# Layer 0 of a diffusion trunk: its first eight projection units on the input before normalisation, and the square sums in the third block

## The chip, the cores and the metric

The kernel runs on one core of one Trainium2 chip. The time is the device time in microseconds (us) of one execution, as a median over several. Five engines work side by side and meet only at semaphores: TensorE (PE, with its weight load PEld), VectorE (DVE), ScalarE (ACT), GpSimd (POOL) and SyncE (SP), which here issues nearly all transfers (DMA).

## The reference, cut to what matters

Two layers run over 128 context tokens and 256 latent tokens, 384 columns in all. Each begins so:

```python
mod = silu(cond) @ w_ada + b_ada              # (2, 6144): one row for each kind of token
sh1, sc1, g1, sh2, sc2, g2 = split(mod, 6)
h = x * rsqrt(mean(x*x) + EPS) * g_norm1 * (1 + sc1) + sh1
u = h @ w_in                                  # columns feed four mixers and their gates
```

Write s for g_norm1 * (1 + sc1), which differs per channel, and r for the reciprocal root, which differs per token. Since r is one number per token, h @ W equals r * ((x*s) @ W) + sh1 @ W. The product can so be made before r is known, if sh1 @ W is computed beside it (two columns, one for each kind of token). All products keep 32-bit accuracy by splitting each operand into a high and a low part and adding three matmuls: high*high, low*high and high*low.

## The kernel before, in words

Channels lie on the 128 partitions, in 8 blocks k of 128; tokens are the 384 free columns. A projection unit is 128 output columns: 8 blocks times 3 matmuls of 384 columns. Layer 0 has 13 mixing units: xa0, xa1, q0, q1, xc0, xc1, k0, k1, then v0 and v1 (made together in `values`, with the token tiles as weights), cq, ckv, cqr. 32 gate units follow.

**The head of layer 0.** Its first 7 units (SKIP) are computed side by side in banks 0 to 6, block by block, as their inputs arrive. For each block j there are two transfers: `start_ada` j (1024 KB of modulation weights: shift and scale of channel block j; 6 buffers, so the seventh waits for a buffer) and `start_raw` j (448 KB, the weights of 7 units for that block). SP issues them alternately, behind the condition, the ones, the input x in two halves, and the small parameters.

PE runs `start_squares` (11 warm-up matmuls on the ones, then the square sums of x in two halves), `start_modulate(0)`, `start_modulate(1)`, then for each j `start_products(j)` (7 high*high, then 14 with a low part) and `start_modulate(j + 2)`. A modulation is 32 matmuls, each with a weight of 32 columns, into bank 7; the trace shows 64 records for it.

DVE squares half of x and adds the squares before it. In `start_norm(j)` it transposes the modulation out of bank 7, adds the bias (`mod`), makes s (`sc1`), multiplies x*s*r into `wide`, splits the weights (`start_low`), and makes the low part of h. ACT squares the other half, computes r from the square sums (`roots`: Ln, then Exp), makes the high part of the weights (`start_high`) and of h (`normed_high`). POOL has nothing to do in the head.

**After the head.** Unit 7 (k1) runs through the general path `dense` on the normalised high and low parts `ahi`, `alo`, and then `values(8)` runs three token tiles. ACT copies the units' sums out of their banks into `proj` and signals `mix_out`; the first tile asks only for one of them, the third for `mix_out` of 8 units in the changed and unchanged code alike. POOL's window sums start on units 0 and 1. The streamed weights pass through 4 buffers (`w_raw` to `w_hi` by ACT, to `w_lo` by DVE).

**Layer 1 already has the scheme of the change.** Its first 8 units run on the unnormalised x*s with two more columns for the shift; `rescale` on DVE multiplies each unit's sums with r and copies the two columns out, `add_shift` on ACT adds them, and POOL multiplies x*s by r for the units that come later (`normed`). Its rows in the trace show what these operations take.

## Time and profile before

| | us |
|---|---|
| median of 3 runs | 1218.28 (1217.79 to 1218.54) |
| the profiled execution's own time | 1218.61 |
| its span | 1216.7 |
| PE busy | 1200.5 (99% of the span) |
| DVE busy | 946.3 (78%) |
| ACT busy | 601.4 (49%) |
| POOL busy | 147.1 (12%) |

The span runs from the first to the last recorded instruction; the execution's own time is 1.9 us more. PE's busy share says only that it had an instruction under way: matmuls overlap, and the step from one start to the next says what one costs. What the order of the work is worth is read from the waits and from the start times.

### The profile page before, as it was taken

What the parts mean: (1) busy time and instruction counts of PE and PEld (TensorE: products, weight loads), DVE (VectorE), ACT (ScalarE), POOL (GpSimd) and SP (SyncE); (2) the same over time, 40 slices, a digit from 0 to 9 for tenths busy, and PEclk for the clock granted to TensorE, in tenths of its full rate; (3) what the DMA queues carried; (4) which work ended last, traced back from release to release, by engine and by line L of the source; (5) the groups of instructions that cost most, each with busy time, mean ns of one, the idle gap of its engine ahead of it and who ended that gap; (6) DMA issues with size and microseconds to landing.
All of it is one profiled execution on the core that took longest, in us unless ns stands there. A gap on an engine that the chain in (4) does not pass through costs nothing.

```text
span 1216.7 us, 19749 instructions
## 1 busy us (share of the span) xinstructions
PE 1200.5 (99%) x7688; PEld 1146.8 (94%) x7688; DVE 946.3 (78%) x1751; ACT 601.4 (49%) x1023; POOL 147.1 (12%) x125
## 2 busy tenths in 40 slices
PE   7999999999999999999999999999999999999998
PEld 6987999989989999999999889999999999999998
DVE  5588877848689999988867978787687899999532
ACT  3445564542365555543446545646437764454321
POOL 0222000008200000000132500000271200000000
PEclk9999999999999999999999999999999999999999
DMA  9763433544744455457673644343325444454443
GB/s 369 295 221 124 145 116 119 173 140 156 259 167 147 156 161 169 155 186 245 217 263 108 222 138 139 105 128 115 104 88 186 144 132 145 156 165 148 138 139 122
DMA packets 53821, 200.91 MB, mean 165 GB/s; under 512 B 6816, under 2 KB 7232, under 8 KB 51936
## 3 DMA queue, kind: packets, MB, share of 16 engines
q1 hardware_dynamic: 53408, 198.96, 48.2%
q8 instruction: 62, 1.02, 0.3%
q0 software_dynamic: 320, 0.69, 0.2%
q14 instruction: 31, 0.25, 0.1%
HBM read 197.35 MB, written 2.27 MB: 164 GB/s over the span
## 4 chain that ended last, share of the span: by engine, by line
PE 95%; DVE 2%; DMA 1%; issue 1%; ACT 0%; SPq 0%; DVEq 0%
PE bank L1602 27%; PE bank L1604 27%; PE bank L1603 27%; PE bank L1920 1%; PE bank L1900 1%; PE bank L1670 1%; DMA start_ada<-start_ada 1%; DVE w_lo L1077 1%; PE bank L1675 1%; PE bank L1674 1%; PE bank L1890 1%; PE bank L1659 1%; PE bank L1875 1%; DMA ada<-ada_w 1%; PE bank L1724 0%
## 5 line engine op out<-in xcount | busy, mean ns | idle before, releaser
L1602 PE MATMUL bank<-act_hi,w_hi 128*128 128x384 f32 x1240 | 421.9, 340 | 0.1
L1604 PE MATMUL bank<-act_hi,w_lo 128*128 128x384 f32 x1240 | 415.0, 335 | 0.0
L1603 PE MATMUL bank<-act_lo,w_hi 128*128 128x384 f32 x1208 | 403.9, 334 | 0.0
L1077 DVE TENSOR_TENSOR w_lo<-w_raw,w_hi 128x1024 fp32r<-128x1024 f32 x251 | 324.5, 1294 | 97.4 <-ACT w_hi L673 96.5
L673 ACT ACTIVATE w_hi<-w_raw 128x1024 fp32r<-128x1024 f32 x251 | 264.2, 1053 | 159.4 <-DMA w_raw<-stream 159.3
L1602 PEld LDWEIGHTS bank<-act_hi,w_hi 128*128 128x128 f32 x1240 | 233.1, 188 | 8.7 <-issue 5.3
L1604 PEld LDWEIGHTS bank<-act_hi,w_lo 128*128 128x128 f32 x1240 | 232.7, 188 | 0.0
L1603 PEld LDWEIGHTS bank<-act_lo,w_hi 128*128 128x128 f32 x1208 | 226.9, 188 | 0.6
L1602 PE MATMUL bank<-mlp_hi,w_hi 128*128 128x384 f32 x352 | 118.3, 336 | 0.0
L1604 PE MATMUL bank<-mlp_hi,w_lo 128*128 128x384 f32 x352 | 118.3, 336 | 0.0
L1603 PE MATMUL bank<-mlp_lo,w_hi 128*128 128x384 f32 x352 | 118.3, 336 | 0.0
L673 ACT ACTIVATE mlp_tmp<-bank,params 128x384 f32<-128x384 f32 x88 | 54.7, 667 | 73.4 <-PE bank L1604 73.1
L1492 DVE SCALAR_TENSOR_TENSOR mlp_tmp<-bank,params,mlp_tmp 128x127 f32<-128x127 f32 (+1 forms) x176 | 64.7, 409 | 16.0 <-ACT mlp_tmp L673 16.0
L1496 DVE SCALAR_TENSOR_TENSOR mlp_tmp<-bank,params,mlp_tmp 128x127 f32<-128x127 f32 (+1 forms) x176 | 65.2, 412 | 3.1
L1602 PEld LDWEIGHTS bank<-mlp_hi,w_hi 128*128 128x128 f32 x352 | 66.2, 188 | 0.1
L1603 PEld LDWEIGHTS bank<-mlp_lo,w_hi 128*128 128x128 f32 x352 | 66.2, 188 | 0.0
L1604 PEld LDWEIGHTS bank<-mlp_hi,w_lo 128*128 128x128 f32 x352 | 66.2, 188 | 0.0
L1108 DVE SCALAR_TENSOR_TENSOR row_products_mix<-ada,cond_spread_mix 128x1024 f32<-128x1024 f32 x44 | 56.4, 1282 | 5.0 <-DMA cond_spread_mix<-cond_rows 3.2
L673 ACT ACTIVATE gates_b<-bank 128x384 f32<-128x384 f32 x48 | 23.6, 492 | 64.0 <-PE bank L1604 63.7
L1363 DVE TENSOR_REDUCE small<-bank 128x1 f32<-128x384 f32 (+1 forms) x72 | 31.2, 462 | 28.3 <-PE bank L1878 11.1
L662 POOL TENSOR_TENSOR wide<-wide 128x768 f32<-128x768 f32 x8 | 18.6, 2330 | 273.7 <-DVE wide L1431 273.7
L1602 PE MATMUL bank<-merged_hi,w_hi 128*128 128x384 f32 x128 | 43.4, 339 | 4.0 <-DVE w_lo L1077 3.6
(261 smaller groups left out, 1866.0 us busy)
## 6 DMA issues: line engine op xcount, KB each, us to landing
w_raw<-stream SPq DMA_DIRECT2D x251, 512.0 KB, 3.7
ada<-ada_rows SPq DMA_DIRECT2D x64, 512.0 KB, 4.7
start_ada<-start_ada SPq DMA_DIRECT2D x8, 1024.0 KB, 17.9
ada<-ada_w SPq DMA_DIRECT2D x8, 512.0 KB, 5.5
ada_norm<-ada_w SPq DMA_DIRECT2D x8, 512.0 KB, 5.8
start_raw<-start_w SPq DMA_DIRECT2D x8, 448.0 KB, 18.5
cond_spread_mix<-cond_rows SPq DMA_DIRECT2D x2, 1024.0 KB, 8.6
cond_spread<-cond_rows SPq DMA_DIRECT2D x2, 1024.0 KB, 7.7
```

What stands on the lines that cost most here:

```text
L662: own(nc.gpsimd.tensor_tensor(g[:, 0:2, :], g[:, 0:2, :], g[:, 2:4, :], ALU.add))
L673: return nc.scalar.activation(out, in_, func, **kw)
L1077: V.tensor_tensor(wlo[s][:, :], raw[s][:, :], whi[s][:, :].bitcast(F32), ALU.subtract).then_inc(lo_ready, 1)
L1108: V.scalar_tensor_tensor(out[:, :], ada[b % 2][:, :], 1.0, tile[:, t, :], ALU.mult, ALU.mult, accum_out=mod[:, at, t:t + 1]).then_inc(rows ...
L1363: own(V.reduce_max(small[:, c + m:c + m + 1], bank[score_bank(i, m)][:, 0:n], AX))
L1492: own(V.scalar_tensor_tensor(f[:, m, a + 1:e], b[:, a:e - 1], before, f[:, m, a + 1:e], ALU.mult, ALU.add))
L1496: ins = V.scalar_tensor_tensor(f[:, m, a:e - 1], b[:, a + 1:e], behind, f[:, m, a:e - 1], ALU.mult, ALU.add)
L1602: T.matmul(out, wb[s][0][:, w, :], hi[k], start=first and k == 0, stop=False)
L1603: T.matmul(out, wb[s][0][:, w, :], lo[k], start=False, stop=False)
L1604: ins = T.matmul(out, wb[s][1][:, w, :], hi[k], start=False, stop=last and k == n - 1)
L1659: ins = T.matmul(bank[7][p0:p0 + STRIP, j * n:(j + 1) * n], conds[:, k, :], w[:, c:c + n], start=k == 0, stop=k == KD - 1)
L1670: T.matmul(outs[u], start_hi[j][:, cols[u]], HI[j], start=j == 0, stop=False)
```

## The change: what it does

- The 7 side-by-side units, and unit 7 behind them, use x*s without r (`suhi`, `sulo`, 386 columns: 384 and the two of the shift). `start_rescale` (DVE) and `start_add_shift` (ACT) finish all 8 units after the head.
- ACT makes x*s (`late`) and its high part, DVE its low part. POOL adds up the squares and then multiplies x*s by r for the later units; ACT and DVE make `ahi`, `alo` of these blocks from the fourth block on (START_NORMED).
- The square sums move on PE from ahead of the head to between the high and the low products of the third block, as one matmul into bank 7 (it was four into bank 4). All squares are ACT's.
- SP issues the parameters and `start_ada` 0 ahead of the input; the input goes in four quarters, with the blocks. `start_ada` has 3 buffers instead of 6.
- PE runs modulation 0, high products 0, modulation 1, low products 0, then modulation 2, high and low products 1, and so on. DVE makes the high weights of block 0, ACT the others. Modulation 4 waits for r, which ACT reads out of the same bank. 10 warm-up matmuls instead of 11.

```diff
-START_ADA = 6
-WARM = 11
+START_ADA = 3
+WARM = 10
+START_UNITS = SKIP + 1
+START_NORMED = {3: (0,), 4: (1, 2), 5: (3,), 6: (4, 5), 7: (6,)}
...
+            def load_input(h):
+
+                c0, c1 = 2 * h * TOK, (2 * h + 2) * TOK
+                sp.dma_start(x_t[:, c0:c1], x_in[:, c0:c1]).then_inc(x_loaded[h], 16)
...
-            for h in range(2):
-                c0, c1 = h * KD // 2 * TOK, (h + 1) * KD // 2 * TOK
-                sp.dma_start(x_t[:, c0:c1], x_in[:, c0:c1]).then_inc(x_loaded[h], 16)
             sp.dma_start(par[:, 0:HEAD_PARAMS], params[0:1, :, 0:HEAD_PARAMS].rearrange("a p n -> (a p) n")
                          ).then_inc(head_par_loaded, 16)
             for j in range(KD):
+                if 1 <= j < KD // 2:
+                    load_input(j)
                 if j >= START_ADA:
                     sp.wait_ge(ada_done, 2 * (j - START_ADA + 1))
                 sp.dma_start(start_ada_buf[j % START_ADA][:, :], start_ada[j:j + 1, :, :].rearrange("a p n -> (a p) n")
                              ).then_inc(start_ada_loaded[j % START_ADA], 16)
+                if j == 0:
+                    load_input(j)
                 sp.dma_start(start_raw[j][:, :], start_w[j:j + 1, :, :].rearrange("a p n -> (a p) n")
...
+                if l == 0:
+                    for h in range(KD // 2):
+                        pool.wait_ge(start_sq, h + 1)
+                        own(nc.gpsimd.tensor_tensor(wide[:, 2 * h, :], wide[:, 2 * h, :], wide[:, 2 * h + 1, :], ALU.add))
+                        own.wait()
+                        if h >= 1:
+                            own(nc.gpsimd.tensor_tensor(wide[:, 0, :], wide[:, 0, :], wide[:, 2 * h, :], ALU.add))
+                            own.wait()
+                    nc.gpsimd.sem_inc(start_sq_sum, 1)
+                    pool.wait_ge(rstd_ready, 1)
+                    for k in range(KD):
+                        pool.wait_ge(start_full, k + 1)
+                        nc.gpsimd.tensor_tensor(wide[:, k, :], late[:, k, :], rsn, ALU.mult).then_inc(norm_full, 1)
...
-            for h in range(2):
-                act.wait_ge(x_loaded[h], 16)
-                A(wide[:, 4 * h:4 * h + 2, :], x[:, 4 * h:4 * h + 2, :], ACT.Square).then_inc(start_sq_act, 1)
...
-                    own(A(rsn, bank[SUM_BANK[n + (l and n)]][:, 0:TOK], ACT.Ln, scale=1.0 / D, bias=EPSC))
+                    sums = bank[SUM_BANK[n + (l and n)]][:, 0:TOK] if l + n else bank[7][:, P:P + TOK]
+                    own(A(rsn, sums, ACT.Ln, scale=1.0 / D, bias=EPSC))
...
+                def start_square(h):
+
+                    act.wait_ge(x_loaded[h], 16)
+                    A(wide[:, 2 * h:2 * h + 2, :], x[:, 2 * h:2 * h + 2, :], ACT.Square).then_inc(start_sq, 1)
+
+                def start_unnormed_high(j):
+
+                    act.wait_ge(start_shift, j + 1)
+                    if j % 2 == 0 and j < 4:
+                        act.wait_ge(x_loaded[j // 2], 16)
+                    for a, e, c in RANGES:
+                        ins = A(late[:, j, a:e], x[:, j, a:e], ACT.Copy, scale=sc1[:, j, c:c + 1])
+                    ins.then_inc(start_full, 1)
+                    A(suhi[:, j, TOK:start_width], mod[:, j, :], ACT.Copy)
+                    act.wait_ge(start_full, j + 1)
+                    A(suhi[:, j, 0:TOK], late[:, j, :], ACT.Copy).then_inc(start_u_hi, 1)
+
+                def start_add_shift(q):
+
+                    out = pj[:, PJ[MIX[q]], :]
+                    act.wait_ge(start_rescaled, q + 1)
+                    for a, e, c in RANGES:
+                        ins = A(out[:, a:e], out[:, a:e], ACT.Identity, bias=start_sums[:, q, c:c + 1])
+                    ins.then_inc(mix_out, 1)
...
-                    norm(0)
-                    for u in range(SKIP, SKIP + 3):
-                        split(u)
+                    for j in range(KD):
+                        if j >= 1:
+                            start_high(j)
+                        if j == KD // 2 - 1:
+                            roots(0)
+                        start_unnormed_high(j)
+                        for h in ((0, 1), (2, 3))[j] if j < 2 else ():
+                            start_square(h)
+                        for k in START_NORMED.get(j, ()):
+                            normed_high(0, k)
+                    split(SKIP)
+                    normed_high(0, KD - 1)
+                    split(SKIP + 1)
+                    split(SKIP + 2)
+                    for q in range(START_UNITS):
+                        start_add_shift(q)
+                        if MIX[q] in SQUARED:
+                            mix_squares(q)
...
-            for h in range(2):
-                dve.wait_ge(x_loaded[h], 16)
-                xs = x[:, 4 * h + 2:4 * h + 4, :]
-                V.tensor_tensor(wide[:, 4 * h + 2:4 * h + 4, :], xs, xs, ALU.mult).then_inc(start_sq_dve, 1)
-                dve.wait_ge(start_sq_dve, h + 1)
-                dve.wait_ge(start_sq_act, h + 1)
-                V.tensor_tensor(wide[:, 4 * h:4 * h + 2, :], wide[:, 4 * h:4 * h + 2, :], wide[:, 4 * h + 2:4 * h + 4, :],
-                                ALU.add).then_inc(start_sq_sum, 1)
...
+                    if l + n == 0:
+                        dve.wait_ge(start_u_lo, k + 1)
...
-                    dve.wait_ge(start_w_hi, j + 1)
...
-                def start_norm(j):
+                def start_unnormed_low(j):
 
                     c0 = j * 2 * STRIP
-                    turned_block = rt_t[:, c0:c0 + 2 * STRIP].rearrange("p (b c) -> p b c", c=STRIP)
+                    turned_block = start_turned_t[:, c0:c0 + 2 * STRIP].rearrange("p (b c) -> p b c", c=STRIP)
                     dve.wait_ge(ada_done, 2 * (j + 1))
-                    turn = V.transpose(rt_t[:, c0:c0 + 2 * STRIP], bank[7][:, c0:c0 + 2 * STRIP])
+                    turn = V.transpose(start_turned_t[:, c0:c0 + 2 * STRIP], bank[7][:, j % 2 * 2 * STRIP:(j % 2 + 1) * 2 * STRIP])
                     if j < KD - 1:
                         turn.then_inc(start_read, 1)
                         dve.wait_ge(start_read, j + 1)
                     else:
                         turn.then_inc(mod_read, 2)
                         dve.wait_ge(mod_read, FROM + 2)
-                    V.tensor_tensor(mod[:, j:2 * KD:KD, :], turned_block[:, :, 0:2],
-                                    pc("b_ada", 0, 2 * KD)[:, j:2 * KD:KD].unsqueeze(2).to_broadcast([P, 2, 2]), ALU.add
-                                    ).then_inc(start_shift, 1)
-                    dve.wait_ge(start_shift, j + 1)
-                    own(V.scalar_tensor_tensor(sc1[:, j:j + 1, :], mod[:, KD + j:KD + j + 1, :], 1.0,
-                                               pc("g1", j, j + 1).unsqueeze(2).to_broadcast([P, 1, 2]), ALU.add, ALU.mult))
+                    own(V.tensor_tensor(mod[:, j:2 * KD:KD, :], turned_block[:, :, 0:2],
+                                        pc("b_ada", 0, 2 * KD)[:, j:2 * KD:KD].unsqueeze(2).to_broadcast([P, 2, 2]), ALU.add))
                     own.wait()
+                    V.scalar_tensor_tensor(sc1[:, j:j + 1, :], mod[:, KD + j:KD + j + 1, :], 1.0,
+                                           pc("g1", j, j + 1).unsqueeze(2).to_broadcast([P, 1, 2]), ALU.add, ALU.mult
+                                           ).then_inc(start_shift, 1)
+                    if j == 0:
+                        dve.wait_ge(start_w_loaded[0], 16)
+                        V.tensor_copy(start_hi[0][:, :], start_raw[0][:, :]).then_inc(start_first_hi, 1)
+                        dve.wait_ge(start_first_hi, 1)
+                    else:
+                        dve.wait_ge(start_w_hi, j)
+                    start_low(j)
+                    dve.wait_ge(start_u_hi, j + 1)
+                    low(sulo[:, j, 0:TOK], late[:, j, :], suhi[:, j, 0:TOK])
+                    low(sulo[:, j, TOK:start_width], mod[:, j, :], suhi[:, j, TOK:start_width]).then_inc(start_u_lo, 1)
+
+                def start_rescale(q):
+
                     dve.wait_ge(rstd_ready, 1)
-                    for a, b, c in RANGES:
-                        ins = V.scalar_tensor_tensor(wide[:, j, a:b], x[:, j, a:b], sc1[:, j, c:c + 1], rsn[:, a:b],
-                                                     ALU.mult, ALU.mult)
-                    ins.then_inc(norm_full, 1)
-                    start_low(j)
-                    dve.wait_ge(norm_hi, j + 1)
-                    for a, b, c in RANGES:
-                        ins = V.scalar_tensor_tensor(alo[:, j, a:b], wide[:, j, a:b], mod[:, j, c:c + 1],
-                                                     ahi[:, j, a:b].bitcast(F32), ALU.add, ALU.subtract)
-                    ins.then_inc(norm_lo, 1)
+                    dve.wait_ge(unit_done, FROM + q + 1)
+                    V.tensor_copy(start_sums[:, q, :], bank[q][:, TOK:start_width])
+                    V.tensor_tensor(pj[:, PJ[MIX[q]], :], bank[q][:, 0:TOK], rsn, ALU.mult).then_inc(start_rescaled, 1)
 
                 if l == 0:
                     dve.wait_ge(head_par_loaded, 16)
                     for j in range(KD):
-                        start_norm(j)
-                    for u in range(SKIP, SKIP + 3):
-                        split(u)
+                        start_unnormed_low(j)
+                        for k in START_NORMED.get(j, ()):
+                            normed_low(0, k)
+                    split(SKIP)
+                    normed_low(0, KD - 1)
+                    split(SKIP + 1)
+                    split(SKIP + 2)
+                    for q in range(START_UNITS):
+                        start_rescale(q)
...
-                    for _ in range(WARM):
-                        T.matmul(bank[6][:, 0:P], cc("ones"), cc("ones"), start=True, stop=True)
-                    for h in range(2):
-                        pe.wait_ge(start_sq_sum, h + 1)
-                        for k in (4 * h, 4 * h + 1):
-                            ins = T.matmul(bank[4][:, 0:TOK], cc("ones"), wide[:, k, :], start=k == 0, stop=k == 5)
-                    ins.then_inc(ss_done, 1)
+                    pe.wait_ge(start_read, KD // 2)
+                    pe.wait_ge(start_sq_sum, 1)
+                    T.matmul(bank[7][:, P:P + TOK], cc("ones"), wide[:, 0, :], start=True, stop=True).then_inc(ss_done, 1)
 
                 def start_modulate(j):
 
@@ -1652,27 +1717,36 @@
                     pe.wait_ge(start_ada_loaded[j % START_ADA], 16 * (j // START_ADA + 1))
                     if j >= 1:
                         pe.wait_ge(start_read, j)
+                    if j == KD // 2:
+                        pe.wait_ge(rstd_ready, 1)
                     n = 2 * STRIP
                     for k in range(KD):
                         for strip in range(4):
                             p0, c = STRIP * strip, (k * 4 + strip) * n
-                            ins = T.matmul(bank[7][p0:p0 + STRIP, j * n:(j + 1) * n], conds[:, k, :], w[:, c:c + n],
+                            ins = T.matmul(bank[7][p0:p0 + STRIP, j % 2 * n:(j % 2 + 1) * n], conds[:, k, :], w[:, c:c + n],
                                            start=k == 0, stop=k == KD - 1)
                     ins.then_inc(ada_done, 2)
 
-                def start_products(j):
-
-                    outs = [bank[u][:, 0:TOK] for u in range(SKIP)]
-                    cols = [slice(u * P, (u + 1) * P) for u in range(SKIP)]
-                    pe.wait_ge(start_w_hi, j + 1)
-                    pe.wait_ge(norm_hi, j + 1)
+                start_cols = [slice(u * P, (u + 1) * P) for u in range(SKIP)]
+
+                def start_high_products(j):
+
+                    if j == 0:
+                        pe.wait_ge(start_first_hi, 1)
+                    else:
+                        pe.wait_ge(start_w_hi, j)
+                    pe.wait_ge(start_u_hi, j + 1)
                     for u in range(SKIP):
-                        T.matmul(outs[u], start_hi[j][:, cols[u]], HI[j], start=j == 0, stop=False)
+                        T.matmul(bank[u][:, 0:start_width], start_hi[j][:, start_cols[u]], suhi[:, j, :], start=j == 0, stop=False)
+
+                def start_low_products(j):
+
                     pe.wait_ge(start_w_lo, j + 1)
-                    pe.wait_ge(norm_lo, j + 1)
+                    pe.wait_ge(start_u_lo, j + 1)
                     for u in range(SKIP):
-                        T.matmul(outs[u], start_hi[j][:, cols[u]], LO[j], start=False, stop=False)
-                        ins = T.matmul(outs[u], start_lo[j][:, cols[u]], HI[j], start=False, stop=j == KD - 1)
+                        out = bank[u][:, 0:start_width]
+                        T.matmul(out, start_hi[j][:, start_cols[u]], sulo[:, j, :], start=False, stop=False)
+                        ins = T.matmul(out, start_lo[j][:, start_cols[u]], suhi[:, j, :], start=False, stop=j == KD - 1)
...
-                    start_squares()
+                    for _ in range(WARM):
+                        T.matmul(bank[6][:, 0:P], cc("ones"), cc("ones"), start=True, stop=True)
                     pe.wait_ge(cond_ready, 1)
                     start_modulate(0)
-                    start_modulate(1)
                     for j in range(KD):
-                        start_products(j)
-                        if j + 2 < KD:
-                            start_modulate(j + 2)
+                        if 1 <= j < KD - 1:
+                            start_modulate(j + 1)
+                        start_high_products(j)
+                        if j == 0:
+                            start_modulate(1)
+                        if j == KD // 2 - 2:
+                            start_squares()
+                        start_low_products(j)
+                    unit_ready(SKIP)
+                    pe.wait_ge(mod_read, FROM + 2)
+                    dense(bank[7][:, 0:start_width], SKIP, range(KD), [suhi[:, k, :] for k in range(KD)],
+                          [sulo[:, k, :] for k in range(KD)]).then_inc(unit_done, 1)
...
-                            if l and t == 0:
+                            if t == 0:
```

What is left out of the diff: the addresses of the new tiles, their semaphores, and ACT's later loop, which now copies sums out of the banks only from unit 8 on.

## Rows read from the trace of the kernel before

**Rows 1.** The page: the chain that ended last, shares of the span by engine.
```profile
PE 95%; DVE 2%; DMA 1%; issue 1%; ACT 0%; SPq 0%; DVEq 0%
```

**Rows 2.** Who PE waited for: us in total, times, longest.
```profile
PE bank L1659 <- DMA start_ada<-start_ada: 1.7, 1, 1.7
```

**Rows 3.** Timeline of PE in the head: start, us, engine, line, operation.
```profile
4.18 4.45 PE L1642 MATMUL bank<-consts 128*128 128x128 f32 x22 [4.18 <-DMA consts<-consts]
...
14.49 1.10 PE L1659 MATMUL bank<-start_ada,cond_silu 128*32 128x64 f32 x64 [1.66 <-DMA start_ada<-start_ada]
15.53 1.48 PE L1670 MATMUL bank<-act_hi,start_hi 128*128 128x384 f32 x7
16.84 0.34 PE L1674 MATMUL bank<-act_lo,start_hi 128*128 128x384 f32 x1
...
19.44 1.10 PE L1659 MATMUL bank<-start_ada,cond_silu 128*32 128x64 f32 x64
...
24.33 1.10 PE L1659 MATMUL bank<-start_ada,cond_silu 128*32 128x64 f32 x64
...
52.25 0.34 PE L1602 MATMUL bank<-act_hi,w_hi 128*128 128x384 f32 x1
```

**Rows 4.** Timeline of SP's transfer queue: input, then modulation blocks 2 and 3.
```profile
1.65 0.90 SPq L474 DMA_DIRECT2D x<-x_in  x2
...
5.37 0.44 SPq L480 DMA_DIRECT2D start_ada<-start_ada  x1
...
6.39 0.44 SPq L480 DMA_DIRECT2D start_ada<-start_ada  x1
```

**Rows 5.** Transfers issued at 4.8, 5.3, 6.3 us; last: us to landing.
```profile
start_raw<-start_w SPq DMA_DIRECT2D x1, 448.0 KB, 10.7
...
start_ada<-start_ada SPq DMA_DIRECT2D x1, 1024.0 KB, 14.0
...
start_ada<-start_ada SPq DMA_DIRECT2D x1, 1024.0 KB, 16.5
```

**Rows 6.** Windows: stretch, us, engines busy, granted clock, DMA share, GB/s.
```profile
14.00:18.00 4.00, 3.51 (x78) 3.42 (x79) 3.90 (x11) 2.25 (x5) 0.00 (x0) 1.00 1.02 413
```

**Rows 7.** Instruction fetches, 16 to 18 us: packets, MB, share of engines.
```profile
q8 instruction: 1, 0.02, 3.2%
```

**Rows 8.** Timeline of DVE in the head: transpose, step behind the scale, weights.
```profile
12.97 0.25 DVE L1192 STREAM_TRANSPOSE rope_tmp<-bank 128x64 f32<-128x64 f32 x1 [2.78 <-PE bank L1659]
...
13.65 0.75 DVE L1208 SCALAR_TENSOR_TENSOR wide<-x,scale,rstd 128x128 f32<-128x128 f32 x2
14.32 1.08 DVE L1184 TENSOR_TENSOR start_lo<-start_raw,start_hi 128x896 fp32r<-128x896 f32 x1
```

**Rows 9.** Timeline of ACT ahead of layer 1: x*s and its high part.
```profile
603.43 0.80 ACT L673 ACTIVATE gated_late<-x,scale 128x128 f32<-128x128 f32 x2 [0.45 <-DVE x L1444]
604.26 0.53 ACT L673 ACTIVATE unnormed_hi<-gated_late 128x384 fp32r<-128x384 f32 x1
```

**Rows 10.** Chain that ended last, 83 to 87 us: square-sum matmul, next one.
```profile
83.92 0.65 PE bank L1764 x2
...
86.05 0.38 PE bank L1602
```

**Rows 11.** Layer 1's units ending: timelines of DVE, ACT and PE.
```profile
657.70 0.54 DVE L1166 TENSOR_TENSOR proj<-bank,rstd 128x384 f32<-128x384 f32 x1
...
659.05 0.79 ACT L673 ACTIVATE proj<-proj,cond_raw 128x128 f32<-128x128 f32 x2
659.87 0.53 ACT L673 ACTIVATE wide<-proj 128x384 f32<-128x384 f32 x1
...
658.14 0.36 PE L1724 MATMUL bank<-w_hi,act_hi 128*128 128x256 f32 x1 [1.08 <-ACT proj L673]
```

**Rows 12.** Layer 1: POOL's eight products, a DVE pair beside them.
```profile
627.00 8.12 POOL L597 TENSOR_TENSOR wide<-gated_late,rstd 128x384 f32<-128x384 f32 x8 [14.98 <-ACT rstd L673]
...
628.91 2.40 DVE L1144 SCALAR_TENSOR_TENSOR act_lo<-wide,mod,act_hi 128x128 fp32r<-128x128 f32 x2 [0.92 <-ACT act_hi L673]
```

36 lines of the change are left out of this document (21 added, 15 removed).

## The prediction, made before the change was run

> **What bounds the kernel now.** I read the page's chain first: it is 95% PE [rows 1]. The reader is to see that time is saved here only by giving PE less to do or by starting it earlier. The waits of PE come second: the one place in the head is a wait of 1.7 us for a modulation block [rows 2]. Third is PE's timeline. From 14.49 on there is no gap: each block takes 4.89 us, from modulation to modulation (19.44 to 24.33), made of 1.04 for a modulation (14.49 to 15.53), 1.31 for 7 high products (to 16.84) and 2.60 for 14 low ones (to 19.44). Unit 7 starts at 52.25 [rows 3]. So the change is worth what it moves the start of this gapless stream, less what it adds to it.
>
> Fourth are the transfers, since they decide how early the stream can start. From 14 to 18 us the DMA share is 1.02 and 413 GB/s flow [rows 6]; the queue is full, and a block lands when the bytes ahead of it have gone. Modulation block 2, issued at 5.37, takes 14.0 us to land: 19.37, while PE asks for it at 19.44. Block 3, issued at 6.39, takes 16.5: 22.89, asked for at 24.33 [rows 3 to 5]. The reader is to see that block 2 has 0.1 us and block 3 only 1.4 us to spare. PE can't be moved far ahead of these two.
>
> **The change part by part.**
>
> *The start.* PE must run the warm-up, modulation 0 and its input chain, high products 0, modulation 1 and low products 0. The 22 warm-up records (11 matmuls) take 4.3 us, so ten end near 8.1 [rows 3]; the modulation ends near 9.3. Then come transpose to scale on DVE, 0.68 [rows 8], x*s with its high part on ACT, 0.80 and 0.53 [rows 9], and some 0.2 for the copy of the shift: high products at 11.6. DVE makes the high weights of block 0 in that time and their low part in 1.08 [rows 8], with no other use for it. Modulation block 1 now has half the input and 448 KB of weights ahead of it as before, 768 KB less: it lands about 13. Low products 0 end near 13 + 1.04 + 2.60 = 16.7. Before, the same work ended at 19.44 [rows 3]. Taken alone this is 2.7 us.
>
> *The limit behind it.* Modulation 2 comes next. Ahead of block 2 (and with it) there were 5608 KB; now the last quarter of the input is behind it, 384 KB, which at 413 GB/s are 0.95 us [rows 6]. Against that the bulk of the stream starts one issue later, because the parameters go first: the two halves of x were issued in 0.90 [rows 4], so one is about 0.47. Block 2 lands at 19.37 - 0.95 + 0.47 = 18.9. Modulation 3 then starts at 18.9 + 4.89 = 23.8. Block 3 has the same bytes ahead of it as before, and lands at 22.89 + 0.47 = 23.4, just in time. So of the 2.7 us only 24.33 - 23.8 = 0.55 are left at modulation 3: the transfers take the rest.
>
> The bound from below: the weights of block 1, 448 KB, landed at 15.57 (issued 4.87, 10.7 later) [rows 5]. The 1024 KB behind them should take 2.5 us at 413 GB/s, and took 3.8; the 1.3 us more fall in with an instruction fetch on one of the 16 engines (3.2% of 16 engines' 2 us are 1.0 us) [rows 7]. Without that lag, and without the late issue, block 2 lands at 19.37 - 0.95 - 1.3 = 17.1 and modulation 3 starts at 22.0 (block 3 is there at 21.6): 2.3 saved. I take the lag as it is, since TensorE's program is nearly the same up to here. The bound from above is a second lag of 1.3 us.
>
> *What PE has more to do behind that point.* One full-precision matmul for the square sums now lies in the third block: two records, 0.65, and the reduced-precision matmul behind such a pair takes 0.38 in place of 0.17, so 0.86 [rows 10]. Ahead of 14.49 the four old ones cost nothing, since PE waited for block 1 anyway. Two more columns on 6 x 21 + 24 = 150 matmuls at 0.17 us for 384 columns are 0.14. Sum: -0.55 + 0.86 + 0.14 = +0.45.
>
> *ACT, DVE and POOL beside PE.* Before modulation 4 ACT must have read the square sums: two passes of 384 columns, each like the 0.53 of [rows 9], so 1.1 us against the 2.60 of the low products that PE has in between. ACT's queue holds the square of the last quarter of x ahead of the high weights of block 2. That quarter is queued just ahead of modulation block 3, so it lands 1024 KB earlier: 23.4 - 2.5 = 20.9. The square, the high weights (each taken as 1.1 us, by DVE's 1.08 for 896 columns [rows 8]) and x*s with its high part (1.5) follow one another: at most 24.6. PE asks for them at 23.8 + 1.04 = 24.8. Covered by 0.2; late is at worst some tenths. SP's waits for the three buffers cost nothing: block 5 of the modulation is issued when modulation 2 is done, near 20, with some 2.5 MB still queued ahead of it.
>
> *The hand-over to unit 8.* ACT used to copy a unit's sums while unit 7 ran. Now DVE rescales (0.54 each) and ACT adds the shift (0.82 each, the wait behind it included) and squares three of the first seven (0.43 more each) [rows 11]; the third tile of `values` waits for all eight. Modulation 7 ends near 45.0 (unit 7's start, 52.7, less two blocks of 1.31 + 2.60). Then 0.7 on DVE and 1.5 on ACT; two pairs of high parts and three weight splits of about 1.2 keep ACT and DVE to about 53.2. The first rescaled unit is there at 53.8, the eighth is finished 8 x 0.82 + 3 x 0.43 = 7.9 later, 61.7. PE: unit 7 ends at 52.7 + 4.2, two tiles of 24 matmuls of 256 columns (about 0.115 each) end at 62.4. So 0.7 us of cover. If it is gone, layer 1 shows what comes: PE waited 1.08 at this very line [rows 11]. I take 0, ends 0 and 1.1.
>
> *The lock between POOL and DVE.* POOL now makes four products of 1.0 us in a row as soon as r is there (8 took 8.12), and beside such a row a pair of DVE's took 2.40, where the like pair in the head took 0.75 [rows 8, 12]. That falls on the low parts of block 3 and so on the scale of block 4, which has about 1 us to spare. I take 0; the ends are 0 and one product, 1.0.
>
> The Trainium skill speaks against this part too: "SBUF — State Buffer", section "SBUF: two separate sides", says that a POOL operation and a DVE one with two inputs in SBUF lock each other out for a whole instruction and don't share. By that rule each of three DVE operations in the row waits up to a full product; the DVE product out of PSUM beside POOL, with a single SBUF input, would be free of it. The trace agrees: 2.40 against 0.75. By the rule the sum would have 0.4 to 1 us on top, if the scale of block 4 comes that much late; by the slack of 1 us, nothing.
>
> **The sum.** The profiled execution took 1218.61, its span 1216.7 and 1.9 around it, which nothing here touches. 1218.61 + 0.45 = 1219.06. It stands 0.33 above the median shown, so the time predicted is 1218.28 + 0.45 = 1218.7. From unit 8 on all is as before: POOL's window sums have a wait of 15 us to give, and the splits of later units had some us of lead.
>
> **The rivals.**
>
> *A: the transfers come earlier.* For it: the block 2 lag may be bound to the moment, not to the queue, and quarters of x are smaller pieces. Against: the bytes ahead of block 3 are the same. With the whole lag and the late issue gone, 2.3 are saved and 1.0 added: -1.3, 1217.0.
>
> *B: new stalls where DVE, ACT and POOL meet PE (the lock, the hand-over).* For it: 1.08 in layer 1 and the 2.40 pair. Against: the slack counted above. One of them in full and part of the other: +0.45 + 1.5, 1220.2. It decides as soon as DVE's scale of block 4 is more than 1 us late, or the last add later than 62.4.
>
> *C: PE's clock falls in the new gaps; slower than before.* PE now has two gaps in its start, about 9.3 to 11.6 (2.3 us, waiting for x*s) and 16.7 to 18.9 (2.2 us, for block 2), where it had one of 1.7. Place and price: if the engine runs at 1.2 GHz after the first gap, the work from 11.6 to 16.7, some 5 us at 2.4, takes twice that and ends near 21.6, past block 2's landing by 2.7: +0.45 + 2.7 = +3.1, 1221.4. For it: the warm-up records take 4.3 us for 11, 0.39 us each, while two records with three times the columns take 0.65 later, so the engine does start at the lower level whatever the granted clock shows. Against: the gap of 1.66 was followed at full pace (1.04 for a modulation, before as later), and granted clock reads 1.00 [rows 3, 6, 10]. It decides from a pace of high products 0 above 0.3 us each.
>
> That the start isn't earlier at all (block 1 late, x*s late) costs nothing up to 2 us, since block 2 decides.
>
> **How the numbers follow.** Forecast 0.57, A 0.18, B 0.17, C 0.08. What a measurement here can tell from no change is 0.2%, 2.4 us: faster is under 1215.8, slower over 1220.7. The forecast's own range is 1218.2 to 1219.3. A in full is -1.3, so only what I can't find would be faster by 2.4: 0.03. C is slower outright, and a third of B, with both stalls in full (1.1 + 1.0 + 0.45 = 2.55): 0.08 + 0.05 = 0.13. The same: 0.84. The range goes down to 1216.9 (A in full) and up to 1220.8 (B in full); it leaves out C and little else.
>
> **What would show it.** In the timeline: high products 0 near 11.6, low products 0 ended near 16.7, then a wait of PE for `start_ada` of about 2 us ending at 18.9; modulation 3 at 23.8; unit 7 at 52.7, and no wait at the first tile of `values`. Wrong would be: modulation 3 before 23 (A), a PE wait for DVE or ACT of over 0.5 us (B), products at 0.3 us each before 19 (C), or a difference that comes from behind 65 us, which I hold to be unchanged.

## The result: 1222.5 us, slower by 0.3%, and the profile after

The changed kernel takes 1222.46 us (median of 6 runs, 1221.90 to 1223.06), the kernel before, beside it on the same chip, 1218.51 (6 runs, 1217.79 to 1219.27). The ratio is 1.003, with a 95% interval of 1.002 to 1.0039: slower by 3.95 us, above the 0.2% that can be told from no change and outside the range of 1216.9 to 1220.8. The profiled execution took 1222.86, its span 1221.1, so 4.4 us more span than before.

The head of the kernel, where the whole change lies, is not where they are. This is the timeline of PE after the change (start, us, engine, line, operation), which answers to [rows 3]:

```profile
3.34 4.64 PE L1774 MATMUL bank<-consts 128*128 128x128 f32 x20 [3.34 <-DMA consts<-consts]
7.90 1.59 PE L1726 MATMUL bank<-start_ada,cond_silu 128*32 128x64 f32 x64
11.83 2.11 PE L1740 MATMUL bank<-start_unnormed_hi,start_hi 128*128 128x386 f32 x7 [2.33 <-ACT start_unnormed_hi L706]
13.87 1.94 PE L1726 MATMUL bank<-start_ada,cond_silu 128*32 128x64 f32 x64
...
18.43 1.10 PE L1726 MATMUL bank<-start_ada,cond_silu 128*32 128x64 f32 x64
...
23.37 1.10 PE L1726 MATMUL bank<-start_ada,cond_silu 128*32 128x64 f32 x64
...
28.92 1.10 PE L1726 MATMUL bank<-start_ada,cond_silu 128*32 128x64 f32 x64
...
33.82 1.10 PE L1726 MATMUL bank<-start_ada,cond_silu 128*32 128x64 f32 x64
...
52.25 0.35 PE L1671 MATMUL bank<-start_unnormed_hi,w_hi 128*128 128x386 f32 x1
```

The reader is to see that the high products of block 0 start at 11.83 (11.6 was predicted), modulation 2 at 18.43, modulation 3 at 23.37 and unit 7 at 52.25, which is to the hundredth where it started before [rows 3]. From modulation 3 (23.37) to modulation 4 (28.92) it is 5.55 us, from there to modulation 5 (33.82) only 4.90: the 0.65 between are the square sums.

The 4.4 us are made far behind. These are windows of PE after the change, 70 us in the middle of the down projection of layer 0 and of layer 1, where PE has no gap; columns: stretch, its us, PE busy and its matmuls, granted clock, DMA share, GB/s.

```profile
540.00:610.00 70.00, 70.00 (x399) 1.00 0.65 220
1135.00:1205.00 70.00, 70.00 (x400) 1.00 0.42 136
```

The same two windows in the kernel before:

```profile
540.00:610.00 70.00, 70.00 (x406) 1.00 0.69 226
1135.00:1205.00 70.00, 70.00 (x405) 1.00 0.46 150
```

Busy 100%, clock 1.00 in both, and yet seven and five matmuls fewer in 70 us after the change: the single product has become dearer. The busy column can't show it; the count can. The rows of the timeline where the down projection of layer 0 begins, and where the first product behind it starts, after the change:

```profile
529.78 0.34 PE L1671 MATMUL bank<-mlp_hi,w_hi 128*128 128x384 f32 x1
...
622.72 0.34 PE L1671 MATMUL bank<-unnormed_hi,w_hi 128*128 128x386 f32 x1
```

92.94 us for 528 products, 176.0 ns each. Before it was 529.33 to 620.91, 91.58 us, 173.4 ns. I read the same from the timelines for every group of products, as the mean step from one start to the next on the same pair of tiles. Products on `act_hi` and `act_lo` take 173.5 in both kernels; those on `mlp`, `branch` and `merged` went from about 173.3 to 176.0.

What these three have in common is their place in SBUF, the memory on the chip in which the kernel lays out its tiles by byte address. The new tile `start_sums_shift`, 16 floats, lies just ahead of `gates_a`, and moves every tile from there on by 64 bytes: `mlp_hi` from 124864 to 124928, `branch_hi`, `branch_lo`, `merged_hi` and `merged_lo` likewise, from 192 modulo 256 to 0. The weight tiles and `act` lie ahead of it and stay at 128 modulo 256. ("192 modulo 256" means that the address leaves 192 when divided by 256.)

The waits of PE after the change (in total, times, longest) answer to [rows 2]:

```profile
PE bank L1774 <- DMA consts<-consts: 3.3, 1, 3.3
PE bank L1671 <- DVE w_lo L1134: 3.0, 4, 1.0
PE bank L1740 <- ACT start_unnormed_hi L706: 2.3, 1, 2.3
...
PE bank L1807 <- ACT proj L706: 1.1, 1, 1.1
PE bank L1826 <- ACT rstd L706: 1.0, 1, 1.0
```

The 1.7 us for `start_ada` are gone, 2.3 for x*s have come. The one at L1807 was there before [rows 11], the 1.0 at L1826, in layer 1, was not. It isn't the head's alone: e1 below shows 0.5 us of it, and e5, the kernel before with moved tiles, 0.9.

### The profile page after: what moved, and what is told of

Its sections match the earlier page's. It is cut to its first block, busy times and chain, and to the rows that moved or that the text cites. A ratio compares the mean times of both kernels' runs of the same rounds, so it can differ in the third digit from the quotient of the medians.

```text
span 1221.1 us, 19811 instructions
## 1 busy us (share of the span) xinstructions
PE 1205.8 (99%) x7680; PEld 1152.8 (94%) x7680; DVE 950.2 (78%) x1764; ACT 614.0 (50%) x1064; POOL 163.8 (13%) x140
## 4 chain that ended last, share of the span: by engine, by line
PE 95%; DVE 2%; DMA 1%; issue 1%; ACT 1%; SPq 0%; DVEq 0%
PE bank L1671 27%; PE bank L1673 27%; PE bank L1672 27%; PE bank L2003 1%; PE bank L1983 1%; PE bank L1740 1%; DVE w_lo L1134 1%; PE bank L1748 1%; PE bank L1749 1%; PE bank L1726 1%; PE bank L1973 1%; PE bank L1958 1%; DMA ada<-ada_w 1%; DVE gated_late L1500 0%; PE bank L1807 0%
## 5 line engine op out<-in xcount | busy, mean ns | idle before, releaser
L706 ACT ACTIVATE mlp_tmp<-mlp_tmp 128x384 f32<-128x384 f32 x44 | 23.1, 526 | 46.9 <-DVE mlp_tmp L1565 46.9
```

The lines of the kernel that those rows point to most:

```text
L706: return nc.scalar.activation(out, in_, func, **kw)
```

## The experiments

The theory after this first reading: the reordered head costs nothing, and the 64 bytes cost all of the 4 us. The rivals were that the reordering disturbs something late in the kernel, and that what costs is the sums' own tile.

### e1: the sums without a tile of their own

The sums go into `bias_next`, a tile of 24 floats that the first layer doesn't need until later. All addresses are then as before, and all instructions as in the changed kernel.

```diff
-        start_sums_t, o = tile("start_sums_shift", 2 * START_UNITS, o)
-        start_sums = start_sums_t[:, :].rearrange("p (q c) -> p q c", c=2)
+        start_sums = bias_t[:, 0:2 * START_UNITS].rearrange("p (q c) -> p q c", c=2)
```

> The changed kernel with one difference: its 16 new floats (the shift sums) lie in a tile that layer 0 doesn't use yet, so everything behind them in SBUF lies where it lay before the change, 64 bytes lower than in the changed kernel. Theory (the 64 bytes cost): matmuls that stream the MLP, branch and merge operands step by 173.5 ns again instead of 176.0, some 1800 of them, and the time falls from 1222.5 by 3.5 to 4.5, to about 1218.5. Rival (the new head shifts the phase of transfers and DVE work in the later stages): addresses change nothing, steps stay at 176.0, time stays at 1222.5 within 0.5.

Measured: 1218.88 us (11 runs, 1217.67 to 1219.90) against 1218.40; ratio 1.0002, interval 0.9993 to 1.001. In the windows of the down projections the count is back:

```profile
540.00:610.00 70.00, 70.00 (x406) 1.00 0.67 226
1135.00:1205.00 70.00, 70.00 (x405) 1.00 0.46 149
```

So of the 3.95 us the address takes 3.6 (1222.46 less 1218.88), and the change that was meant is worth no difference that can be measured.

### e2 and e3: other distances

```diff
-        top = o
+        top = o + 128        # e2; + 32 in e3
```

> The kernel of e1 with everything from the first gate tile on 128 bytes higher: these operands then start at 64 modulo 256 (e1: 192; changed kernel: 0). If only a start at a multiple of 256 is slow, the MLP operands step by 173.5 and the time is that of e1. If any shift from the old place is slow, or a start at 0 or 64 modulo 128 decides, they differ: by modulo 128 they would be as e1, 173.5, so a step of 176 here says that it is the distance from the old place.

> The kernel of e1 with everything from the first gate tile on 32 bytes higher, so that operands start at 224 modulo 256 and at 32 modulo 64. If a start at a multiple of 64 is all that counts, or a boundary is crossed inside a row, the step rises above 176; if only a start at a multiple of 128 or 256 is slow, it stays at 173.5.

Measured: e2 1219.47 (one run), with 173.3 ns on `mlp`, but 176.5 on `merged` in layer 0 and 174.3 in layer 1, 174.1 to 174.8 on `branch`. e3 1222.98 (one run), 176.7 on all of them. It isn't any move that costs, and 64 bytes aren't special: by the steps, 128 bytes more than in e1 are nearly free, and 32 bytes cost most.

### e5: the kernel before, moved by 32 bytes; e6: the 64 bytes without the tile

e5 is the kernel before with `top = o + 32` and nothing else. e6 is e1 with `top = o + 64`.

> The kernel before with one edit: everything from gates_a on moved up by 32 bytes (so that mlp_hi, branch_hi and merged_hi start at 224 modulo 256 instead of 192); no instruction is added, removed or reordered. Address theory: a step of 176 to 177 ns for the 384-column products on these tiles, as in the changed kernel with the same 32 bytes (176.7), for some 912 products a layer: 1824 x 3.2 ns = 5.8 us at most, and as in the pair e1 and e3 some 4 us: 1222 to 1223 us. Rival (it needs the reordered head as well, for example another phase of the transfers against the products): 1218.4, as the kernel before.

> The changed kernel with its sums in bias_next (as e1) and 64 bytes of nothing ahead of gates_a, so every address from there on is that of the changed kernel, while the sums' tile itself is gone. Address theory: the changed kernel's time, 1222.0 to 1222.9 us, step of mlp products 176.0. Rival (the sums' own tile costs, by its place or by who reads and writes it, and the addresses don't): 1218.9 as e1.

Measured: e5 1223.07 (5 runs, 1222.56 to 1223.69) against 1218.66, ratio 1.0034, interval 1.0021 to 1.0047. e6 1222.36 (5 runs, 1222.20 to 1225.25), ratio 1.0036, interval 1.0022 to 1.005. The kernel before loses 4.4 us by 32 bytes of nothing. Its windows, one in the down projection and one where `act` is read:

```profile
540.00:610.00 70.00, 70.00 (x399) 1.00 0.65 219
1000.00:1070.00 70.00, 70.00 (x406) 1.00 0.45 151
```

399 as after the change, and 406 on the tile that didn't move. e6 has the changed kernel's time and its 176.0 ns without the sums' tile. Both rivals have fallen: the reordering isn't needed for the loss, and neither is the tile.

### e7: the weights moved by 128 bytes

So far "address of the moving tile" and "its distance from the weights" were one and the same, since the weights never moved. Here they do.

```diff
         raw, whi, wlo = [], [], []
+        o += 128
         for s in range(SLOTS):
```

> e1 with 128 bytes ahead of the weight tiles, and the tiles behind them moved with them by 128, less what is put back ahead of gates_a: w_hi and w_lo start 128 bytes later, act_hi and act_lo stay. If what counts is where the moving tile stands relative to the weights, the products on act_hi and act_lo (173.5 ns before) slow down: 1218 + 3500 x 2.6 ns = 1227 us. If only the moving tile's own address counts, act stays at 173.5, and mlp and branch, now at 96 modulo 256 (32 modulo 64), go to 176.7 as in e3: 1223 us.

Measured: 1226.93 (one run). `w_lo` and `w_hi` stand at 0 modulo 256, and `mlp_hi` came to 124992, 64 modulo 256; the 96 that I had written was a slip. At 64 `mlp` ran at 173.3 in e2 as well, so here `mlp` doesn't tell the two theories apart; `act` does. The products on `act`, at an unchanged address, went from 173.5 to 175.9 ns (175.7 in layer 1), those on `mlp`, `branch` and `merged` ran at 173.3 to 173.5. The same windows, now with one in the stream of `act`:

```profile
540.00:610.00 70.00, 70.00 (x406) 1.00 0.68 228
1000.00:1070.00 70.00, 70.00 (x400) 1.00 0.46 150
```

The loss has changed sides: 406 where it was 399, and 400 in the window that holds 406 in e1 and e5. 3664 products on `act` by 2.2 ns are 8.1 us, and 1226.93 less e1's 1218.88 is 8.05.

### e9: the weights moved by 64 bytes, the rest at the changed kernel's addresses

```diff
         raw, whi, wlo = [], [], []
+        o += 64
         for s in range(SLOTS):
```

The sums are in `bias_next`, as in e1, so that from `gates_a` on every tile is where the changed kernel has it.

> e1 (the changed kernel with its sums in bias_next) with 64 bytes of nothing ahead of the weight tiles: w_lo, w_raw and w_hi start at 192 modulo 256 instead of 128, and everything from gates_a on stands at exactly the addresses of the changed kernel (mlp_hi at 124928, 0 modulo 256); act_hi and act_lo stay at 128. After e7 (where moving the weights alone by 128 took the products on act from 173.5 to 175.9 ns at an unchanged address) two theories: (a) the distance from the weights to the moving tile counts, modulo 256: 128 is slow, 0 and 64 are fast. Then mlp, branch and merged (distance 64) run at 173.3 though they stand where they ran at 176.0 in the changed kernel; the products on act are at distance 192, where e2 showed 173.3 for mlp and 174 to 176.5 for merged and branch: 1218.5 to 1221 us, nearest 1219. (b) The moving tile's own address counts, and what slowed act in e7 was something else: mlp at 176.0, act at 173.5, 1222.4 us.

Measured: 1222.28 (5 runs, 1221.22 to 1225.63), ratio 1.0034, interval 1.0021 to 1.0047. `mlp_hi` stands at 124928 as in the changed kernel, and its products take 173.3 ns where there they took 176.0; `branch` and `merged` 173.6. `act`, now at distance 192, takes 174.5.

```profile
540.00:610.00 70.00, 70.00 (x405) 1.00 0.67 223
1000.00:1070.00 70.00, 70.00 (x403) 1.00 0.45 148
```

405 and 403, against 399 and 406 after the change. So the absolute address is out, and the distance from what was moved is in. What was moved in e7 and e9 is more than the weights' high and low parts: `w_raw`, where their transfers land, has the same start as `w_lo`, and all small tiles up to `gates_a` went along. That it is the weight operand of the product, and none of these, is the plainest reading; no run separates them.

The time was above my range all the same: `act` has more products than all others together, so 3664 by 0.9 are 3.3 us, close to the 3.4 between the medians of e9 and e1. In e9's profile a fall of the clock in the head adds 1.5 (below); its span is 4.2 above e1's.

### e10: distance 0

e1 with `top = o + 192`.

> e1 with 192 bytes ahead of gates_a: the moving tiles from there on at 128 modulo 256, as the weights and act are, so at distance 0. Distance theory: 173.4 to 173.9 on mlp, branch and merged, 1218 to 1219.5 us. Rival (any move away from the addresses before costs): 176 and 1222.

Measured: 1219.51 (one run), `mlp` 173.3, `branch` 173.6, `merged` 173.5. The steps are as expected, and the time stands at the upper end. Its profile has the same fall of the clock as e9's: granted clock 0.57 from 20 to 24, and 6.47 us from modulation 2 to 3. Where layer 1's down projection begins, e10 is 0.8 us behind e1. All that was read, as the mean step in ns; the distance is the start of the moving tile less that of the weight tile, modulo 256:

```
distance   moving tile (kernel)                                 step
   0       act (all but e7, e9); mlp, merged, branch (e10)      173.0 to 174.2
  64       mlp, branch, merged (before, e1, e7, e9)             172.7 to 174.1
  96       mlp, branch, merged (e3, e5)                         176.4 to 177.1
 128       mlp, branch, merged (after, e6)                      175.4 to 177.0
 128       act (e7)                                             175.0 to 176.8
 192       mlp (e2)                                             173.0 to 174.0
 192       act (e9)                                             174.4 to 174.7
 192       merged, branch (e2)                                  174.1 to 176.9
```

### e11: the 386-column blocks at a wider pitch

The streams on the unnormalised inputs have 386 columns, so their blocks lie 1544 bytes apart (the pitch) and stand at all multiples of 8; they run at 177.4 ns in the kernel before too. If that were due to the distance, aligning the blocks would give a kernel better than both.

```diff
-            t, at = tile(f"unnormed_hi{n}", KD * wide_w, at, F32R)
+            t, at = tile(f"unnormed_hi{n}", KD * wide_ws[n], at, F32R)      # (wide_w, 416); unnormed_lo likewise
```

> e1, with the blocks of the second unnormalised input of layer 1 (386 columns) 1664 bytes apart instead of 1544, so that each stands at distance 64 or 192 from the weights instead of at all multiples of 8. Distance theory: of the 384 products on unnormed in layer 1 those of this tile (half) go from 177.4 to about 174.3 ns (two columns more than 384 are 0.8 ns): 192 x 3.1 = 0.6 us less, 1217.8 to 1218.4 us. Rival (the 177.4 come from the two more columns and from what stands beside them): 177.4 and 1218.9 as e1.

Measured: 1218.62 (11 runs), ratio 1.0001, interval 0.9992 to 1.001. The tile with the wider pitch went from 177.4 to 176.7 ns, not to 174.3; the other stayed at 177.4. So the wider pitch gives back 0.7 of the 4 ns. Of the rest, 0.9 is what two more columns take at the pace of 173.4 for 384. The other 2.4 are open, but the start address has a part: at the old pitch both tiles ran at 176.4 to 176.5 in e2 and at 176.2 in e10, against 177.4 in e1. Whether that adds to the 0.7 of the pitch isn't shown. There is no version here that beats both kernels.

### e4, e8, e12: filling the gap, and the clock

Nine matmuls of ones behind modulation 0 fill the gap of 2.3 us ahead of the first high products, to see whether the clock falls without it. All three runs are e1 with this one edit.

```diff
+                        if j == 0:
+                            for _ in range(FILL):
+                                T.matmul(bank[6][:, 0:P], cc("ones"), cc("ones"), start=True, stop=True)
```

> The kernel of e1 with nine more full-precision matmuls on the ones between modulation 0 and high products 0, to fill TensorE's wait of 2.3 us. Theory: the granted clock no longer falls to half between 12.4 and 15.8 us, low products 0 end near 16.7 and not 18.4, and then block 2 of the modulation is waited for, which lands at 18 or a little before: modulation 2 starts 0 to 0.5 us earlier than in e1 and the time falls by as much. Rival: the low clock set the start of modulation 2 and the block was there long before: 1.5 us less than e1.

> The same kernel as e4 (e1 with nine products of ones behind modulation 0), for a second profile. Its eleven times stood in two groups: 1218.1 to 1219.6 at a mean granted clock of 1.0, and 1221.4 to 1221.9 at 0.998 to 0.999. Clock theory: where the clock falls for some 3.4 us while TensorE has work without a wait behind it, half of the work of that time is lost (1.7 us) and the transfers no longer hide it: a profile with a dip is at 1221 to 1222, one without at 1218 to 1219. Rival (the two groups come from late in the kernel, and the clock only goes with them): a dip and 1218, or no dip and 1221.5.

> The kernel of e4 and e8 once more, for a profile in which the clock falls. Clock theory: with a fall of some 3.4 us in it the time is 1221 to 1222, and the profile shows modulation and high products of the first layer at half speed with no wait of TensorE behind them that takes it up; without a fall 1218 to 1220.5. Rival: a fall and 1218 to 1220, or none and 1221.5.

Measured: e4 1221.41 (11 runs, 1218.12 to 1221.90), ratio 1.0017, interval 1.0008 to 1.0026; e8 1220.31, e12 1219.14 (one each). All three profiles show a granted clock of 1.00 from end to end. In e4's the high products 0 start at 12.04, 1.1 later than in e1, and modulation 2 at 18.75 all the same:

```profile
12.04 1.47 PE L1740 MATMUL bank<-start_unnormed_hi,start_hi 128*128 128x386 f32 x7
...
18.75 1.10 PE L1726 MATMUL bank<-start_ada,cond_silu 128*32 128x64 f32 x64 [1.55 <-DMA start_ada<-start_ada]
```

A stream that starts 1.1 us later waits 1.55 for block 2 where e1's waited 2.02: the landing decides. The 1.1 aren't the filler's. In e4's profile modulation 0 took 1.77 us and the warm-up 4.63, against 1.10 and 4.20 in e1, though the granted clock reads 1.00 there; with the same filler e8 and e12 start these products at 10.71 and 10.92, and modulation 2 at 18.58 and 18.87.

Filling gains nothing, and the median of e4 is 2.5 us above e1's. The thirteen times of this kernel stand in two groups: the seven at a mean clock of 1.0 take 1218.12 to 1220.31, the six at 0.998 or 0.999 take 1221.41 to 1221.90. None of the three profiles caught an execution of the second group, so where those 3 us are lost is open. That they are the clock's is an inference from the means, and a lower mean doesn't do it by itself: eight of e1's eleven runs have 0.998 or 0.999 too, and take 1217.67 to 1219.86. The spread within the first group does show a place: PE waits 1.8 us for ACT's `proj` in layer 1 in e12, 2.3 in e4 and 3.0 in e8, with spans of 1217.3, 1217.8 and 1218.5 (e1: 1.2 and 1216.9). Why the filler would lengthen this wait isn't shown.

Where a fall costs is shown elsewhere. After the change it came behind the first gap, from 12 to 16 us, and e9 had it from 20 to 24. Windows of PE, after the change and then e9 (stretch, us, PE busy, granted clock, DMA share, GB/s):

```profile
12.00:14.00 2.00, 2.00 (x15) 0.60 1.07 436
14.00:16.00 2.00, 2.00 (x65) 0.55 1.04 434
18.00:24.00 6.00, 6.00 (x132) 1.00 1.03 426
```

```profile
18.00:20.00 2.00, 1.34 (x66) 1.00 1.07 448
20.00:24.00 4.00, 4.00 (x16) 0.57 1.02 421
```

At 12 to 16 the products run at the lower of the two levels, 1.2 GHz, for most of the time. Nothing is lost: e1 has the full clock there (2.4 GHz) and then waits 2.02 us for block 2, the changed kernel doesn't wait at all, and both start modulation 2 within 0.2 us (18.60, 18.43). The other profiles agree: the six with a fall ahead of modulation 2 (after, e2, e3, e6, e7, e11) start it at 18.43 to 18.94, the four with none in the head (e1, e4, e8, e12) at 18.58 to 18.87. At 20 to 24 there is no wait behind the fall. This is the timeline of e1, then of e9:

```profile
18.60 1.10 PE L1725 MATMUL bank<-start_ada,cond_silu 128*32 128x64 f32 x64 [2.02 <-DMA start_ada<-start_ada]
...
23.54 1.10 PE L1725 MATMUL bank<-start_ada,cond_silu 128*32 128x64 f32 x64
```

```profile
18.66 1.10 PE L1726 MATMUL bank<-start_ada,cond_silu 128*32 128x64 f32 x64 [2.08 <-DMA start_ada<-start_ada]
...
25.12 1.10 PE L1726 MATMUL bank<-start_ada,cond_silu 128*32 128x64 f32 x64
...
30.68 1.10 PE L1726 MATMUL bank<-start_ada,cond_silu 128*32 128x64 f32 x64
```

It is 6.46 from modulation 2 to 3 where e1 took 4.94: 1.5 us lost, and still there where layer 0's products on `act` begin (67.69 against 66.27). The engine had waited 2.08 us for block 2 just before it; e1 had nearly the same waits in its profile, and no fall. When the clock falls is not derived here.

## Why the prediction was wrong, step by step

**The start: right, within the spread.** High products 0 were predicted at 11.6; 11.83 was measured, and 10.94 in e1. Modulation 1 took 1.94 in place of 1.10 after the change, at the lower clock.

**The limit behind it: right, and the main point of the head.** Block 2 was to let modulation 2 start at 18.9; it starts at 18.43, 18.60 in e1, with a wait of 2.02 there, 18.75 with the filler. In the changed kernel's own profile the predicted wait of 2 us isn't there: low products 0 ran until 18.43 at the lower clock, so the block had landed by then, 0.5 earlier than predicted. Modulation 3 came at 23.37 (23.8 predicted), so 0.96 us were gained against 24.33 [rows 3] instead of 0.55.

**The added work: right as a sum, both terms off.** From modulation 3 to 4 it is 5.55, 0.65 over the 4.90 that follow; 0.86 was predicted for the square sums. Unit 7 starts 0.45 us earlier than the predicted 52.7. Two more columns cost more than their length, though: 176.3 ns a product where `act` took 173.4, so the 150 products of that term by 2.9 are 0.4 us, where I had 0.14.

**The lock between POOL and DVE: it occurs, and costs nothing.** POOL's row of four products after the change, then DVE ahead of it and beside it:

```profile
27.78 4.25 POOL L634 TENSOR_TENSOR wide<-gated_late,rstd 128x384 f32<-128x384 f32 x4 [3.65 <-ACT rstd L706]
```

```profile
24.47 0.15 DVE L1137 TENSOR_TENSOR start_unnormed_lo<-mod,start_unnormed_hi 128x2 fp32r<-128x2 f32 x1
...
28.98 1.20 DVE L1137 TENSOR_TENSOR start_unnormed_lo<-gated_late,start_unnormed_hi 128x384 fp32r<-128x384 f32 x1 [2.80 <-ACT start_unnormed_hi L706]
30.11 0.97 DVE L1137 TENSOR_TENSOR start_unnormed_lo<-mod,start_unnormed_hi 128x2 fp32r<-128x2 f32 x1
31.00 1.57 DVE L1203 SCALAR_TENSOR_TENSOR act_lo<-wide,mod,act_hi 128x128 fp32r<-128x128 f32 x2
...
32.96 0.16 DVE L1260 SCALAR_TENSOR_TENSOR scale<-mod,params 128x2 f32<-128x2 f32 x1
```

0.97 us for an operation on two columns, which took 0.15 at 24.47 with POOL idle, is nearly all waiting. The rule of the Trainium skill that the prediction names ("SBUF — State Buffer", section "SBUF: two separate sides") says the same, and this trace agrees by that 0.97. The scale of block 4 is there at 33.1, ACT's high part made from it follows, and the high products that need it start at 34.85, without a wait.

**The hand-over: right.** PE shows no wait for ACT or DVE at layer 0's `values`. DVE has rescaled the last unit at 57.4, and ACT's last add ends at 60.7, where I had 61.7 for the eighth unit.

**Rival C had the mechanism and not the price.** The clock did fall behind the new gap, and high products 0 took 2.04 us for seven, 0.29 each, in place of 0.19. I had priced the fall at 2.7 us, because by my sum products at half pace would overrun the landing of block 2; the fall ended early enough, and the wait took it up.

**"From unit 8 on all is as before": this is the step that failed.** By it the sum puts nothing on everything behind the hand-over. Of the instructions it is nearly true. The addresses are not as before, and I never looked at them: I went through what the change issues, and not through what it allots. In the change it is one line, 64 bytes. What it cost, by the runs: 1056 products on `mlp` by 2.7 ns are 2.8 us, and the two down projections measure 1.4 us each; 704 on `branch` and `merged` by 2.7 are 1.9, of which 0.6 are taken up by PE's waits for `w_lo` (3.0 in place of 3.6). Together 4.1, against a measured 3.6 between the medians of the changed kernel and e1 and 4.2 between the spans of their profiles.

With the addresses as before, e1, the forecast of 1218.7 meets 1218.88. That they lie so close is partly luck. In e1 unit 7 starts 0.21 us later than before (52.46 against 52.25) where the sum had 0.45, made of terms that were each off; and e1's eleven runs scatter by 2.2 us. The prediction did name what would refute it, a difference from behind 65 us; nothing in the sum or the rivals had a price for it.

What is shown is that moving these tiles by 32 or 64 bytes, with nothing else changed, costs 3.5 to 4.4 us (e6 against e1, e5 against the kernel before). What stays open is why the distance counts at all. The step on `merged` at distance 192 was 176.5 in one layer and 174.3 in the other, with `merged` at the same address, so distance modulo 256 isn't the whole of it. And PE's wait for ACT's `proj` in layer 1 moved between 1.1 and 3.0 us in profiles of kernels with the same addresses from `gates_a` on (before, e1, e4, e8, e12), which I can't derive.

## What to carry to other kernels

A change has a part that isn't in its instructions: where it puts its tiles. Before costing a diff, list the start addresses of the operands that the bounding engine streams, before and after, with their distance from each other modulo 256. If they have moved, put the new small tile where it moves nothing, as e1 did with a tile that was free at the time, and measure that version too. And in a comparison within 0.3%, first count the bounding engine's instructions in a window where it is busy throughout and its granted clock reads the same, in both kernels: if the counts of like instructions differ there, the single instruction has changed its pace, and the order of the work isn't the place to look first.

## What the runs showed of the hardware

- At 384 columns a product takes 172.7 to 174.2 ns with the moving tile at 0 or 64 bytes, modulo 256, from the weight tile, 175.0 to 177.0 at 128, 176.4 to 177.1 at 96. At 192 it is 173.0 to 176.9, by tile and layer. The difference is about 1.5% of a product; with the 3664 products on `act` at 128 it came to 8 us of 1220 (e7, one run). The distance is taken from the start of the weight tile; tiles that moved together with it aren't told apart.
- A stretch at the lower clock of 1.2 GHz cost what the engine wouldn't have waited anyway: 0 us at 12 to 16 (after), with a transfer to wait for behind it, 1.5 us at 20 to 24 (e9, e10), with none. In these kernels PE had waited over 2 us shortly before.
- A granted clock of 1.00 in the first 9 us of a profile doesn't mean full pace: modulation 0 took 1.77 us in e4 and 1.10 in e1, both at 1.00.
- 386 columns instead of 384 cost 3 to 4 ns a product, at either pitch.
- A DVE operation on two columns with both inputs in SBUF took 0.97 us beside a row of POOL's products, and 0.15 with POOL idle.
